# The first head pair of a gated DeltaNet stage in its usual order, with the compression's pages and weights loaded into the projection's ring, and a reordered mask in the merged attention

## What is computed

```python
def compress_blocks(kv, pe, w1, w2):
    sub = kv[:, :n_sub * CMP_STRIDE].reshape(b, n_sub, CMP_STRIDE, g, dh)
    first = jnp.einsum('bnsgd,sdh->bngh', sub + pe[0], w1[0])
    second = jnp.einsum('bnsgd,sdh->bngh', sub + pe[1], w1[1])
    return jax.nn.silu(first[:, :-1] + second[:, 1:]) @ w2
```

```python
_, idx = lax.top_k(imp, top_n)                     # blocks 0 and the last are always kept
s = q . keys(idx) * scale - slopes * dist
p_sel = masked_softmax(s, dist >= 0)
```

## Time and profile before

| | us |
|---|---|
| median of 3 runs | 1650.67 (1647.61 to 1668.31) |
| the profiled execution | 1640.47 |
| its span, first to last instruction | 1638.8 |
| PE busy in it | 1491.6 (91%) |
| DVE, ACT, POOL busy | 953.9, 804.0, 303.6 |
| mean granted TensorE clock | 0.957 |
| first pair of the core, roughly | 219 to 292 |
| merged attention's loop, roughly | 1117 to 1336 |

### The profile page before, as it was taken

One profiled execution on the slowest core, in us unless ns is written; L12 is line 12 of the kernel. 1 busy time (PEld: TensorE's weight loads), 2 busy tenths in 40 slices (PEclk: granted clock), 3 DMA queues, 4 the chain that ended last, 5 costly groups with the idle time before them and its releaser, 6 DMA issues. The chain is left out here.

```text
span 1638.8 us, 37162 instructions
## 1 busy us (share of the span) xinstructions
PE 1491.6 (91%) x13614; PEld 1318.8 (80%) x13614; DVE 953.9 (58%) x1788; ACT 804.0 (49%) x1581; POOL 303.6 (19%) x492
## 2 busy tenths in 40 slices
PE   6999959999989999899999999987777869999895
PEld 6999957777767777589999999965555559999895
DVE  5798542655555456565777743535666656777531
ACT  5766615565546555543544432225555544444431
POOL 0342034243453332200000001032121100000000
PEclk9999978999999999889999999998999979999998
DMA  7764243434552533525555758555444415555640
GB/s 167 248 195 149 78 103 65 102 66 101 96 117 60 100 70 76 135 77 154 142 141 154 182 132 206 161 177 161 159 153 155 140 65 146 139 152 150 159 107 32
DMA packets 287586, 211.97 MB, mean 129 GB/s; under 512 B 29455, under 2 KB 279343, under 8 KB 287040
## 3 DMA queue, kind: packets, MB, share of 16 engines
q1 hardware_dynamic: 278198, 178.42, 41.9%
q0 software_dynamic: 9248, 31.80, 6.9%
q10 hardware_dynamic: 42, 0.44, 0.1%
HBM read 187.76 MB, written 22.85 MB: 129 GB/s over the span
## 5 line engine op out<-in xcount | busy, mean ns | idle before, releaser
L621 PE MATMUL psum<-h_rounded,weights_low 128*128 128x320 f32 x1248 | 392.3, 314 | 1.5 <-DVE weights_low L597 1.5
L623 PE MATMUL psum<-h_rounded,weights_high 128*128 128x320 f32 x1248 | 386.7, 310 | 0.0
L622 PE MATMUL psum<-weighted_x_low,weights_high 128*128 128x320 f32 x864 | 266.6, 309 | 0.0
L621 PEld LDWEIGHTS psum<-h_rounded,weights_low 128*128 128x128 f32 x1248 | 234.7, 188 | 7.6 <-issue 2.4
L623 PEld LDWEIGHTS psum<-h_rounded,weights_high 128*128 128x128 f32 x1248 | 234.6, 188 | 0.0
L597 DVE TENSOR_TENSOR weights_low<-sbuf_resident,weights_high 128x2048 fp32r<-128x2048 f32 x90 | 205.6, 2286 | 30.6 <-ACT weights_high L582 30.4
L582 ACT CAST weights_high<-sbuf_resident 128x2048 fp32r<-128x2048 f32 x90 | 169.9, 1892 | 88.4 <-PE psum L623 58.9
L1253 ACT COPY sbuf_resident<-psum 64x256 f32<-64x256 f32 x256 | 108.5, 424 | 155.9 <-PE psum L1192 153.6
L622 PEld LDWEIGHTS psum<-weighted_x_low,weights_high 128*128 128x128 f32 x864 | 165.4, 191 | 0.2
L696 DVE SCALAR_TENSOR_TENSOR sbuf_stages<-sbuf_stages,sbuf_resident 128x344 f32<-128x344 f32 (+1 forms) x184 | 105.5, 573 | 44.6 <-ACT sbuf_stages L678 40.8
L678 ACT ACTIVATE sbuf_stages<-sbuf_stages,sbuf_resident 128x336 f32<-128x336 f32 (+1 forms) x76 | 44.1, 581 | 165.2 <-DVE sbuf_stages L1972 164.1
(11 more groups left out here) (448 smaller groups left out, 3078.9 us busy)
## 6 DMA issues: line engine op xcount, KB each, us to landing
sbuf_resident<-in_ffn_w_up_dram SPq DMA_DIRECT2D x88, 512.0 KB, 4.8
sbuf_resident<-in_gdn_w_in_dram SPq DMA_DIRECT2D x48, 512.0 KB, 4.9
sbuf_resident<-in_ffn_w_down_dram SPq DMA_DIRECT2D x32, 704.0 KB, 5.9
sbuf_resident<-in_cache_nsa_kv_dram SPq DMA_DIRECT2D x256, 64.0 KB
sbuf_stages<-in_state_gdn_s_dram POOLq DMA_DIRECT2D x16, 512.0 KB, 8.6
out_gdn_s_sample_dram<-sbuf_stages SPq DMA_DIRECT2D x16, 512.0 KB, 3.8
sbuf_resident<-in_gdn_w_out_dram SPq DMA_DIRECT2D x16, 512.0 KB, 5.2
sbuf_stages<-in_cache_nsa_kv_dram POOLq DMA_DIRECT2D x64, 128.0 KB, 3.3
```

Source lines behind the costliest of these rows:

```text
L621: pe.matmul(out, w_lo, x_hi_tile, start=first, stop=False)
L622: pe.matmul(out, w_hi, x_lo_tile, start=False, stop=False)
L623: return pe.matmul(out, w_hi, x_hi_tile, start=False, stop=last)
```

## The change

Three things, in the words of the code.

1. **Layout and loads.** The eight weight pieces become separate places in the ring's slots, each with the unit count after which it is free (third entry of `W1_LOW` and `W1_HIGH`); pages half 0 lies in slot 0 (free after unit 21), half 1 over `hT` (free after unit 24). SP loads piece 0 after unit 18, pages half 0 after 21, pieces 1 and 2 after 22, 3 and 4 after 23, pages half 1 and pieces 5 to 7 after 24. Each piece is loaded with two transfers in place of one. POOL splits pieces 0 to 3 inside `gdn_in` (ahead of its `stage_closed`), piece 4 just behind, and 5 to 7 inside the first pair, each ahead of the low rows of the same tile. Piece 7 is split in two halves, that is, with four instructions in place of two.
2. **Order of the first pair.** All `if first` branches go; tile 0 is turned by PE behind its own drain in `gdn_in`, and ACT copies tile 0 and tile 1 ahead of the pair's first exponent.
3. **Merged attention.** `dve_rank` ends with two instructions more: `ends` copies the bias of the first and last block into `ss`, `bias` writes bias plus penalty of the 14 blocks between. `ssel` then adds the scores to what `ss` holds, and `spen` goes. The pages are loaded in two halves with a semaphore each: half 0 when turn 2 has read it, half 1 when turn 3 has; turns 0 and 1 wait for their own half.

The diff, cut to its core (all removed `first` branches have the form shown):

```diff
-        w1 = space.take(2, 16, CHID, off=at)
-        raw = [space.take(8, KV_DIM, off=at + x * 8 * KV_DIM) for x in range(2)]
+        slot_at = [ring_at + j * SLOT for j in range(RING)]
+        gap_at = [a + KD * 256 for a in slot_at]
+        gap_end = [a + 2 * CHID for a in gap_at]
+        columns_at = idle_at + KD * T
+        raw = [space.take(8, KV_DIM, off=at) for at in (slot_at[0], idle_at)]
+        RAW_FRESH = (21, 24)
+        W1_LOW = [(columns_at, CHID, 18), (second(1), CHID, 22), (second(3), CHID, 22), (third(1), CHID, 23),
+                  (third(3), CHID, 23), (gap_at[0], CHID, 24), (gap_at[2], CHID, 24), (gap_end[0], SLOT, 24)]
+        W1_HIGH = [(second(0), CHID, 22), (second(2), CHID, 22), (third(0), CHID, 23), (third(2), CHID, 23),
+                   (idle_at + 8 * KV_DIM, CHID, 24), (gap_at[1], CHID, 24), (gap_at[3], CHID, 24), (gap_end[2], SLOT, 24)]
...
-                sp.dma_start(w1[:, 0].rearrange("p (a c) h -> p c a h", a=2)[:, m], rows[m]).then_inc(w1_piece_in[m], 16)
+                for a in range(2):
+                    sp.dma_start(half_of(w1[m], a), rows[m][:, a, :]).then_inc(w1_piece_in[m], 16)
...
-            sp.wait_ge(unit_done, UNITS["gdn_in"][1])
-            for m in range(2):
+            sp.wait_ge(unit_done, W1_LOW[0][2])
+            load_w1(0, 0)
+            sp.wait_ge(unit_done, RAW_FRESH[0])
+            load_raw(pages, 0, 0)
+            for m in range(1, 5):
+                sp.wait_ge(unit_done, W1_LOW[m][2])
                 load_w1(0, m)
-            load_raw(pages, 0, 0)
-            for m in range(2, 8):
+            sp.wait_ge(unit_done, RAW_FRESH[1])
+            load_raw(pages, 0, 1)
+            for m in range(5, 8):
                 load_w1(0, m)
-            load_raw(pages, 0, 1)
...
         def pe_core(pe):
             pe.sem_inc(S5["pe"].sem, S5["pe"].first)
-            pe.sem_inc(C["pe"].sem, C["pe"].first - 1)
...
-            if not first:
-                turn_rows(pe, i, 1)
-                fill(0, 1)
+            turn_rows(pe, i, 1)
+            fill(0, 1)
...
-            if first:
-                turn_rows(pe, i, 0, first=True)
-                turn_rows(pe, i, 1)
-                fill(0, 4)
-                turn_rows(pe, i, 2, first=True)
-                fill(4, 6)
-            else:
-                fill(20, 22)
+            fill(20, 22)
...
+            copy_turned_rows(act, 0, 0, first=True)
             act_core_pair(act, 0, 0, 0, "first")
...
-            if not first:
-                copy_turned_rows(act, i, 1)
+            copy_turned_rows(act, i, 1, none_follow=("s_prev",) if place == "first" else ())
             for h in range(2):
                 act.wait_ge(pe_steps.sem, pe_steps.count(f"rows{h}", i))
-                if not first:
-                    act.wait_ge(S5["pool"].sem, S5["pool"].all_before(i))
+                act.wait_ge(S5["pool"].sem, S5["pool"].all_before(i))
...
+            pool.wait_ge(w1_piece_in[m], 32 * (v + 1))
+            if v == 0:
+                pool.wait_ge(unit_done, W1_HIGH[m][2])
...
-                if split:
+                if split or is_first and m >= 5:
                     split_w1(pool, v, m)
...
                 for g in range(NPG):
+                    if half_free is not None and g % 4 == 0:
+                        half_free(g // 4)
                     src = kv_rows[bass.ds(pages[g], 1)].rearrange("o s c -> (o s) c")
-                    pool.dma_start(k_sel[:, g, :], src[:, K_SEL]).then_inc(k_in, 16)
+                    pool.dma_start(k_sel[:, g, :], src[:, K_SEL]).then_inc(k_in[g // 4], 16)
...
-                if n == 0:
-                    pe.wait_ge(k_in, 128 * (it + 1))
+                if n < 2:
+                    pe.wait_ge(k_in[n], 64 * (it + 1))
...
+                dve.tensor_copy(ends(ss[:, 0:PAST]), ends(table("bias_sel"))).then_inc(a.sem, a.step("ends"))
+                dve.wait_ge(a.sem, a.count("pen", it))
+                dve.tensor_tensor(middle(ss), middle(table("bias_sel")), pen.unsqueeze(2).to_broadcast([P, n14, SELB]), ALU.add).then_inc(a.sem, a.step("bias"))
...
-                dve.tensor_tensor(ss[:, 0:PAST].rearrange("p (a b) -> p a b", a=2), psum[:, X_BANK[0]:X_BANK[1] + 1, :], table("bias_sel", 2), ALU.add)
+                dve.wait_ge(A["dve"].sem, A["dve"].count("bias", i))
+                dve.tensor_tensor(scores, psum[:, X_BANK[0]:X_BANK[1] + 1, :], scores, ALU.add)
...
-                dve.tensor_tensor(blocks, blocks, pen.unsqueeze(2).to_broadcast([P, n14, SELB]), ALU.add).then_inc(ds.sem, ds.step("spen"))
-                dve.wait_ge(ds.sem, ds.count("spen", i))
...
             pe.drain().then_inc(stage_closed, 2)
+            pe.sem_inc(C["pe"].sem, C["pe"].first - 1)
+            turn_rows(pe, 0, 0, first=True)
             pe.wait_ge(stage_closed, 4 * 3)
...
+            for m in range(4):
+                split_w1(pool, 0, m)
             pool.drain().then_inc(stage_closed, 2)
-            for m in range(8):
-                split_w1(pool, 0, m)
+            split_w1(pool, 0, 4)
             pool.wait_ge(stage_closed, 4 * 3)
```

More of the change, by code:

```diff
@@ L1073, in build, with piece, half_of @@
         at = idle_at
-        w1 = space.take(2, 16, CHID, off=at)
-        w1_low, w1_high = (rounded(name, space.take(16, CHID, off=at + x * 16 * CHID)) for x, name in ((0, "w1_low"), (1, "w1_high")))
-        at += 2 * 16 * CHID
-        raw = [space.take(8, KV_DIM, off=at + x * 8 * KV_DIM) for x in range(2)]
-        at += 16 * KV_DIM
+        slot_at = [ring_at + j * SLOT for j in range(RING)]
+        gap_at = [a + KD * 256 for a in slot_at]
+        gap_end = [a + 2 * CHID for a in gap_at]
+        columns_at = idle_at + KD * T
+        assert SLOT - KD * 256 >= 3 * CHID and ring_at - columns_at >= 2 * CHID + 4 * DH
+        raw = [space.take(8, KV_DIM, off=at) for at in (slot_at[0], idle_at)]
+        RAW_FRESH = (21, 24)
+        second, third = (lambda x: slot_at[1] + 2 * CHID * x), (lambda x: slot_at[2] + 2 * CHID * x)
+        W1_LOW = [(columns_at, CHID, 18), (second(1), CHID, 22), (second(3), CHID, 22), (third(1), CHID, 23),
+                  (third(3), CHID, 23), (gap_at[0], CHID, 24), (gap_at[2], CHID, 24), (gap_end[0], SLOT, 24)]
+        W1_HIGH = [(second(0), CHID, 22), (second(2), CHID, 22), (third(0), CHID, 23), (third(2), CHID, 23),
+                   (idle_at + 8 * KV_DIM, CHID, 24), (gap_at[1], CHID, 24), (gap_at[3], CHID, 24), (gap_end[2], SLOT, 24)]
+        def piece(start, apart):
+            if apart == CHID:
+                return [space.take(2 * CHID, off=start)]
+            return [space.take(CHID, off=start + a * apart) for a in range(2)]
+        w1 = [piece(start, apart) for start, apart, _ in W1_LOW]
+        w1_low, w1_high = ([[rounded(f"{name}{m}{a}", part) for a, part in enumerate(piece(start, apart))]
+                            for m, (start, apart, _) in enumerate(places)] for name, places in (("w1_low", W1_LOW), ("w1_high", W1_HIGH)))
+        def half_of(parts, a):
+            return parts[0][:, a * CHID:(a + 1) * CHID] if len(parts) == 1 else parts[a]
+        at = slot_at[3]
         TURNED = 2
@@ L1086, in build @@
         at += 4 * NC2
-        w2_cmp = space.take(4, DH, off=at)
-        at += 4 * DH
-        assert at <= cut
+        w2_cmp = space.take(4, DH, off=columns_at + 2 * CHID)
+        assert at <= gap_at[3] and slot_at[3] + SLOT <= cut and 8 * KV_DIM + 2 * CHID <= KD * T
         ck_stage = space.take(2, NC2, off=gconv_at)
@@ L1207, in hidden_part @@
                     pe.wait_ge(S5["pool"].sem, low_rows_count(m, u))
[L1208 removed]
+                weights = half_of((w1_low if part == "low_weights" else w1_high)[m], half)
                 rows = (turned_low if part == "low_rows" else turned_high)[m % TURNED][:, 8 * half:8 * half + 4 * NC2]
[L1210 removed]
+                last = pe.matmul(psum[:, H_BANK[t], 0:4 * NC2], weights[:, t * P:(t + 1) * P], rows,
                                  start=(m == 0 and half == 0 and part == "low_weights"), stop=(m == 7 and half == 1 and part == "low_rows"))
@@ L1389, in pe_core_pair @@
                     last.then_inc(pe_steps.sem, pe_steps.step(f"y{k}{h}"))
-                if k == SMALL and not first:
+                if k == SMALL:
                     turn_rows(pe, i, 6)
-                elif k == SMALL:
-                    fill(8, 11)
             for h in range(2):
@@ L1400, in pe_core_pair @@
             for h in range(2):
-                if h == 0 and first:
-                    fill(13, 16)
-                    turn_rows(pe, i, 5)
-                    fill(16, 17)
-                elif h == 0:
+                if h == 0:
                     fill(24, 25)
-                if h == 0:
                     pe.wait_ge(pool_steps.sem, pool_steps.count("kmask", i))
@@ L1713, in split_w1 @@
         def split_w1(pool, v, m):
-            part = lambda ap: ap.rearrange("p (a c) h -> p c a h", a=2)[:, m]
-            if v:
```

(16 more changed lines are left out.)

98 lines of the change are left out of this document (29 added, 69 removed).

## The result

| | before | after |
|---|---|---|
| median of the runs | 1649.14 (4 runs, 1646.17 to 1668.31) | 1629.51 (4 runs, 1624.09 to 1631.82) |
| ratio, 95% interval | | 0.987 (0.9835 to 0.9906) |
| profiled execution | 1640.47 | 1631.82 |
| first pair, exponent to exponent | 75.3 | 56.0 |
| pair 4, exponent to exponent | 61.45 | 66.25 |

Predicted were 1631 us and less than 2%; measured are 1629.5 and, by the ratio, 1.3%. An execution more than 1.5% above the fastest of its kernel counts in the medians and not in the ratios. A second time, beside its variants, the same kernel gave 1632.37 (6 runs, ratio 0.9863, 0.9816 to 0.991). The two profiled executions, though, differ by only 8.65 us. Before's was faster than all four of its runs in the table, after's the slowest of its four. Part of this document is where the other 11 went.

A forecast was written before the change was run, and what follows sets the result against it. The prediction took late weight pieces, holding up POOL, ACT and PE in the first pair, as the bound. Core 16.6 plus merged attention 3.4 made 20.0 us, from a median of 1650.67 to 1631 us; range 1612 to 1645.

The forecast's parts named there:

- The first exponent: First pair of the core: ACT copies tiles 0 and 1 first, so its first exponent comes at about 226.4, 3.7 us later.
- pieces 3 and 4: Early weight loads, issued at 210.6: landing taken as 3 to 4 us; with 8.8 the stage closes some 2 us late.
- The pair: First pair, exponent to exponent: runs like pair 1, 53.0 us instead of 75.3; 18.6 gained after the later start.
- POOL beside DVE: First pair: POOL's split of piece 6 slows four DVE instructions and PE waits, 1.4 us lost; bounds 0 and 5.7.
- The clock at 222: PE's idle stretch before the first pair: even chance the clock falls, costing up to 2 us; 0.6 taken as loss.
- Core 16.6: Gain of layout, loads and first-pair order together: 18.6 less 1.4 for POOL beside DVE and 0.6 for the clock.
- The second weight load: Weights loaded again for pair 4, with 16 issues for 8: passed during pair 3, so no cost taken.
- What bounds the kernel: First pair: ACT idles 20.06 us for POOL's splits, which wait for weight pieces behind 16 page transfers; excess 22.3 us.
- Merged attention, 3.4: Merged loop: page wait of 1.3 us an iteration goes, DVE's tail eats 0.87; 0.4 gained each, 3.4 over 8.
- Instruction fetch: Rival: PE still waits by "issue" in the first pair, 4.87 us plus some 2 of low clock; 1638 us, chance 0.17.
- pages half 1 of the first pair: Rival "slower": PE stops at tile 4 for these pages; free until 239, at 263 the kernel takes 1655 us; chance 0.02.
- The total, 20: Whole kernel: 16.6 from the core plus 3.4 from the merged attention, 20.0 us gained; chance of the summed forecast 0.62.

The follow-up runs named there:

- split_ahead: After, but POOL splits weight piece 6 together with piece 5, in the first pair and in pair 4; median 1631.09 us, ratio to before 0.9914.
- half_early: After, but SP loads pages half 1 of pair 4 ahead of weight piece 6 and the stores of pair 3; median 1632.62 us, ratio to before 0.9897.
- core_only: Before with the first two parts of the change alone (layout and loads, order of the first pair); median 1636.32 us, ratio to before 0.9916.
- four_fixes: After with pages half 1 of pair 4 earlier, piece 6 split with 5, pieces 1 to 3 split behind POOL's drain, first pair's states later; 1625.35 us, ratio to before 0.9821.
- loads_only: Before with new layout, early loads and early splits, but old order of the first pair and old merged attention; median 1658.12 us, ratio to before 1.0043.
- mixed_only: Before with the third part of the change alone (merged attention), the core unchanged; median 1647.63 us, ratio to before 0.9975.
- keys_only: Before with only the keys' pages of the merged attention loaded in two halves; median 1649.32 us, ratio to before 0.9999.
- after_again: After unchanged, run once more beside its variants on one chip; median 1632.37 us, ratio to before 0.9863.

## Why the prediction was right, point by point

- *The first exponent, 226.4.* 225.87 in after, 225.50 to 227.01 in six others with early loads and usual order. Right, except for the 230.42 of split_ahead. I had priced pieces 3 and 4, at 3 to 4 us with 8.8 as the bound; piece 3, issued at 209.87 in after, was there when POOL came to it at 214.88. What can be late is piece 1, which I didn't price: its issue stands directly behind the 16 page transfers and it took 6 to 12 us. The row behind page transfers was the nearer one for it. In after POOL had 1.25 us to spare before the stage closed.
- *The pair, 53.0.* 52.96 without the split on DVE's copies and with a full clock. Right.
- *POOL beside DVE, 1.4.* 1.5 by split_ahead. Right. The bound of 5.7 did not come true: at the splits of pieces 5 and 7 PE has no wait over 1 us.
- *The clock at 222, even chance, 0.6.* It didn't fall there in seven of eight executions with the usual order and the early loads; it did in split_ahead, where PE stood for 3.67 us. But it fell at other holes: at 251 behind L1378 in after (56.04 against 53.0 + 1.5, so another 1.5), at 239 in half_early (63.73 - 56.0 - 2.27 = 5.4 us). The step that failed is "so a fall costs up to 2 us": I had priced about four times the work of four turns, ahead of a wait that would hide it. In a pair filled to 90% no such wait comes, and all work in the low stretch shows.
- *Core 16.6.* 16.1 by the exponents, 13.9 by the runs of core_only (7 to 21). Right in size.
- *The second weight load, "I take nothing".* Four kernels with the old layout have pair 4 at 61.20 to 61.77, six with the new one at 60.37 to 66.25, mean 62.87, so 1.4 more (the kernels in which pages or split of pair 4 are moved left out). The page wait is no longer for it: 0.76 to 3.97 in these six, 2.65 to 3.75 in the four. In after it is the clock around the wait that takes the time. Whether the layout shifts this or chance does stays open. What I missed is larger: pair 4 takes 54.17 in four_fixes, 7 us less than in before and more than that below after. Moving the page load, which stood behind eight weight pieces and the stores, is enough for 58.40. That before would gain the same from it wasn't tried.
- *What bounds the kernel.* Here the text was wrong and the sum right. ACT's 20.06 us wait stood in the earlier trace rows beside the cause, but taking it away (loads_only) changed nothing. The cause was PE's order, which loads_only shows with 77.59 us. The sum came out because the excess of 22.3 us over a usual pair is the same whatever causes it, and the change also made the order usual.
- *Merged attention, 3.4.* 4.1 by mixed_only; 0.43 an iteration at full clock where I had 0.4. The working wasn't right, and that the sum met it is luck: I had 1.3 less 0.87 for DVE's tail. The tail is there, the window exponent comes 17.26 us behind the output's addition in after and 16.58 in keys_only, 0.68 later. DVE's wait ahead of the window scores is gone, as forecast, in the iterations at full clock; it stays in two iterations of after, 1.8 us in all. But without the tail the gain is 0.5 too, and not 1.3. A releaser's wait is not what is won by removing it; the next wait was 1.2 us at the same group.
- *The rivals.* Instruction fetch came true in part, with a wait of 0.9 to 2.3 us by "issue" in four of eight executions; that it is a fetch stays a theory. PE never waited for pages half 1 of the first pair. The median 10 us above the profiled execution was the right place to start from.
- *The total, 20.* The two pairs of medians differ by 19.6 and 20.5. That it is this close is partly luck: the parts measured alone make 18.0, the intervals reach 6 us and more to either side, and pair 4, where I had taken nothing, lost 1.4 us on average and 4.8 in the profiled execution.

## What to carry to other kernels

An engine's longest wait next to a late datum is not yet the cause: ask what its waiters would do if the datum were there, or try it, as the two halves of a change can be worth nothing each and 14 us together. In a kernel whose queue passes bulk weights, look for the small load behind them that the next stage wants first. Where PE is filled to 90%, count for each hole also the work that the low clock behind it slows, and compare kernels at equal granted clock.

## What the runs showed of the hardware

- *The clock falls at different holes in identical code.* after and after_again are one program. Their iteration of the merged loop took 26.20 us with the clock at 1.00 in one execution and 27.24 with 0.94 in the other; iterations of 28.1 (0.88) and 30.9 (0.78) occur too, and so nearly equal from one kernel with both edits to the next that they look like a few fixed patterns:

```profile
1150.45:1176.65 26.20, 20.40 (x290) 14.89 (x289) 17.63 (x47) 15.07 (x45) 5.05 (x9) 1.00 0.50 160
```

```profile
1145.47:1172.71 27.24, 21.86 (x290) 16.18 (x289) 17.63 (x47) 15.07 (x45) 5.05 (x9) 0.94 0.49 153
```

  The loop as a whole took from 187.8 to 203.3 us between the first and the last output addition, a spread of 15.5 us where the third part of the change gives 4.1. The Trainium skill (TensorE: Matmul & The Clock Gate, What's actually happening) says that the gate's watch is free-running. Two executions of one program with 1.00 and 0.94 in the same iteration are what that would give; where the watch stood in either no run shows.
- *The price of the clock.* 0.01 of mean clock is 33 us at the low level in a span of 1640 (the low level being half), and 9.1 us of time. So a microsecond at the low level costs about 0.28 here on average. In the packed first pair it costs more: half_early's has a mean clock of 0.87, that is some 17 us at the low level, and after's 0.97, some 3 to 4, so 5.4 us for about 13, or 0.4. These are estimates.
- *POOL beside DVE.* Four products of DVE with both inputs in SBUF take 3.86 us beside a cast and a subtract of POOL and 2.37 without. One by one: the third takes 1.61 us beside POOL's subtract (1.32), and the fourth, of the same size with POOL idle, 0.54.
- *A landing time has a spread.* The same two transfers of 128 KB, behind 16 of 64 KB, took 6.1 us from first issue to use in one execution and 11.9 in another.
